# Last feed-forward layer of the first block in two halves of 256 tokens, the second interleaved with the expert rows

## The chip, the cores and the metric

One core of a Trainium2 chip runs the whole kernel. The metric is device time in microseconds. The runs shown took 3353.31, 3354.09 and 3354.44 us (median 3354.09); the profiled execution spans 3351.2 us from its first to its last instruction, 2.9 us less than the median.

## The reference

A model in fp32 on 512 tokens of width 1024. Two layers of a first block (a short convolution, then an SSD mixer, each followed by a SwiGLU layer of inner width 2816), then one hybrid layer (banded attention beside a gated delta rule, then product-key experts). What matters here:

```python
def swiglu_ffn(h, w_in, w_out):            # w_in 1024 x 5632, w_out 2816 x 1024
    gate, up = jnp.split(h @ w_in, 2, axis=-1)
    return (jax.nn.silu(gate) * up) @ w_out
# first block, end of each layer:
h = rmsnorm(x, norm_g[i, 2]) * (1.0 + scale) + shift
y = swiglu_ffn(h, f_w_in[i], f_w_out[i])
x = x + gate * rmsnorm(y, norm_g[i, 3])
# hybrid layer: x -> attention + delta rule -> x, then experts (16 of 16384 for each of 8 heads):
s1, s2 = ...                               # scores against 128 + 128 sub-keys, top 16 of each,
top_s, pos = lax.top_k(cand_s, 16)         # then top 16 of the 256 sums, for each head
u, vv = expert_down[experts], expert_up[experts]
act = jax.nn.gelu(jnp.einsum("thkd,td->thk", u, hb))
y = jnp.einsum("thk,thkd->td", gates * act, vv)
```

Attention and the delta rule look backwards only, so tokens 0 to 255 can pass through the hybrid layer before tokens 256 to 511.

## The kernel before

Activations stand transposed in SBUF: `xT` holds 8 tiles of 128 features x 512 tokens. Each engine has one program written out in order (`pe_program`, `act_program`, `dve_program`, `pool_program`, `sp_program`, L2522 to L2615); semaphores tie them together. There is no planner: the order of the generators' steps is the order of the work.

**Weights in pieces.** A piece is 128 x 1024 words (0.52 MB). SP loads all of them in one fixed order (`LOADS`, L382 on) into four raw slots; a slot is loaded again when its last reader has finished. Among the pieces up to the last feed-forward layer stand 144 loads of modulation weights, of late one to every two pieces; VectorE multiplies them by a vector (`dve_ada`). For the first block a piece is split in two fp32r parts: ACT copies it to a rounded tile (`act_ahead`, L400), VectorE subtracts that copy (`dve_ahead`, L412), three tiles of each deep. `pe_gemm` (L461) then runs 24 matmuls a piece: high x high, high x low, low x high for each of its 8 tiles. The hybrid layer takes its pieces in fp32 straight from the raw slots (`pe_plain`), and for each half of 256 tokens, so these pieces are loaded twice.

**The last feed-forward layer** (`pe_pre`, `pe_ffn`, `pe_out` with index 3): norm over all 512 tokens, 44 gate and up pieces with 512 moving columns, the gated products of all 22 inner tiles kept in SBUF in two parts, then 22 pieces' worth of output weights in the order output tile by output tile (24 shorter pieces), each output tile squared and copied out while the next one is computed. GpSimd adds the squares up (`pool_out`).

**The hybrid layer by halves.** `pe_main(e, f)` (L2240) and its ACT and VectorE counterparts are generators: norm 8 steps (for f = 1 only 2, as the root is computed beforehand by `act_norm_squares`, `pool_norm_sum`, `pe_norm_sum`, `act_norm_root`), projections 15, attention with the delta rule's projections 34 (for f = 1: 16 steps attention alone, then both), inverses 18, state 6, delta norm 5, output projection 9, norm 8, queries and key scores 20. Half 0 runs alone. In its last steps VectorE begins to rank chunk 0 (a chunk is 128 tokens; `dve_topk`, 33 steps a chunk).

**The expert rows.** 512 rows: row n takes one expert for each of the 128 tokens of a chunk, 128 rows a chunk. GpSimd gathers a row's down and up weights (1.05 MB) by an indirect DMA into a ring of slots (`pool_gather`, L2336): 7 slots, from row 150 on 4 more (memory of attention and delta rule, once free), from 260 on one more. VectorE takes the dot with the token (L187, 1024 wide), ACT applies Gelu and the gate and builds a diagonal matrix, TensorE adds the weighted up row to PSUM banks 0 and 1 (`pe_add`, two fp32 matmuls of 512 columns, four records); for rows chosen by `own_add` VectorE adds instead (`dve_add`). A slot is free when its row is added.

**The interleave.** Before the rows, `before_rows` (L2453) does 9 ranking steps and 6 steps of half 1. Then, behind every second row, `steps_of` (L2460) makes one step of half 1 and in chunk 0 one or two ranking steps for chunk 1; when half 1 is through, ranking steps alone. On each engine a row's work and a step's work stand in one queue:

```python
for g, (c, grp) in enumerate(ALL_GROUPS):      # pe_experts
    ...
    if grp % 2:
        steps_of(c, grp // 2, main, ranks)
        next(late, None)
    if g:
        pe_add(e, *ALL_GROUPS[g - 1])
```

Half 1 has 117 steps, so its last step stands at row 222.

Line numbers in the profile are those of small helpers: L153 all matmuls, L164 all activations, L170 two-operand VectorE and GpSimd operations, L182 multiply-adds with a scalar, L187 the dots, L216 the gathers.

Of the kernel before, what the change touches and what calls it, by code (L numbers as in the profile page):

```python
# [226 lines left out]
def build(nc, t, out):  # L227
    ctx = ExitStack()
    with ctx:
# [53 lines left out]
        w_f, w_r = take_r(6144, LOW + 8192)  # L283
        raw_first = raw + [h_mem[:, 4096 + 1024 * i:5120 + 1024 * i] for i in range(4)]
# [38 lines left out]
        def ffn_pieces(layer, half):  # L323
            for kk in range(KF):
                for part in range(2):
                    piece(("ffn", half, kk, part), t["fin"][layer, 2 * kk + part])
            out_pieces(half, t["fout"][layer], FGROUPS)

        ffn_pieces(0, 1)
# [6 lines left out]
        ffn_pieces(1, 3)  # L336
        NSPLIT = len(PIECES)
        for f in range(2):
            for n in range(12):
                piece(("qkv", f, n), t["win2"][n])  # L340
# [9 lines left out]
        NP = len(PIECES)  # L350

# [26 lines left out]
        def w_tile(p):  # L378
            i = 2048 * (p % 3)
            n = 128 * PIECES[p][1]  # L380
            return i, n

        def sp_load(e, i):
            kind, n = LOADS[i]
            s = slot_of(i)
            if former(i) >= 0:
                old, m = LOADS[former(i)]
                if old == "w":
                    e.wait_ge(*(w_lo.at(m) if m < NSPLIT else gemm.at(m)))
                else:  # L390
                    e.wait_ge(*ada_step.at(m))
# [8 lines left out]
        def act_ahead(e):  # L400
            p = nxt["act"]
            if p >= NSPLIT:
                return
            nxt["act"] += 1
            i, n = w_tile(p)
            e.wait_ge(*w_in.at(("w", p)))
            if p >= 3:
                e.wait_ge(*gemm.at(p - 3))
            e.act(w_r[:, i:i + n], raw[slot_of(NUMBER["w", p])][:, 0:n], ACT.Copy).then_inc(*w_hi.tick(p))

        def dve_ahead(e):
            while nxt["dve"] < len(LOADS):  # L412
# [6 lines left out]
                if p >= NSPLIT:  # L419
                    return  # L420
                i, n = w_tile(p)
                e.wait_ge(*w_hi.at(p))
                e.tt(w_r[:, i + 1024:i + 1024 + n], raw[slot_of(a)][:, 0:n], w_f[:, i:i + n],
                     ALU.subtract).then_inc(*w_lo.tick(p))
# [36 lines left out]
        def pe_gemm(e, p, o, rhs, k0=0, start=True, stop=True, ready=None, own=None):  # L461
            i, n = w_tile(p)
            k = n // 128
            hi, lo = tiles(w_r[:, i:i + n], k), tiles(w_r[:, i + 1024:i + 1024 + n], k)
# [765 lines left out]
        mixd = H[:, 0:4, :]  # L1230
        Sst = room(512)
        qT = tiles(room(1024), 4)
        kT, vtok = [tiles(room(2048), 4) for _ in range(2)]
        over = room(8704)
        htk = [room(1024) for _ in range(2)]
        fin_out = room(1024)
        lvl = tiles(room(896), 7)
# [24 lines left out]
        SB = [over[:, 2048:4096], over[:, 0:2048]]  # L1262
        nine = lambda a: [a[:, 512 * i:512 * i + 512] for i in range(9)]
        kv_mem = tail[:, 3584:7680]
# [26 lines left out]
        n1_sq, n1_add, n1_pe = [signal(n) for n in ("half_squares", "half_sum", "half_total")]  # L1291
# [36 lines left out]
        def x_half(i, f, k):  # L1328
            return x_new(3, k) if i == 4 else ps.done(("wo", f, k))
# [28 lines left out]
        n1_sum, n1_log = fin_out[:, 0:512], fin_out[:, 512:768]  # L1358
        n1_part = [fin_out[:, 512:1024], n1_sum]

        def act_norm_squares(e):
            for m in range(4):
                e.wait_ge(*x_half(4, 1, 2 * m + 1))
                if m > 1:
                    e.wait_ge(*n1_add.at(m - 1))
                e.act(pairs(n1_part[m == 0]), xT[:, 2 * m:2 * m + 2, half_of(1)], ACT.Square).then_inc(*n1_sq.tick(m))

        def pool_norm_sum(e):
            for m in range(1, 4):
                e.wait_ge(*n1_sq.at(m))  # L1370
                if m > 1:
                    e.wait_ge(*n1_add.at(m - 1))
                e.tt(n1_sum, n1_sum, n1_part[0], ALU.add).then_inc(*n1_add.tick(m))

        def pe_norm_sum(e):
            o = ps.claim("n1", HB)
            e.wait_ge(*ps.vacant("n1"))
            e.wait_ge(*n1_add.at(3))
            e.mm(o[:, 0:256], ones, n1_sum[:, 0:256], True, False)
            e.mm(o[:, 0:256], ones, n1_sum[:, 256:512], False, True).then_inc(*n1_pe.tick(0))  # L1380

        def act_norm_root(e):
            e.wait_ge(*n1_pe.at(0))
            e.act(n1_log, ps["n1"][:, 0:256], ACT.Ln, bias=cc("eps"), scale=1.0 / D).then_inc(*ps.release("n1"))
            e.wait_ge(*ps.done("n1"))
            e.act(n1_log, n1_log, ACT.Exp, scale=-0.5).then_inc(*rs_ok.tick(("tn", 4, 1)))

        def act_norm_shift(e):
            for s in range(2):
                for k in range(4 * s, 4 * s + 4):  # L1390
                    e.wait_ge(*dve_b.at(("tn", 4, 1, k)))
                    e.act(hrows(k), hrows(k), ACT.Identity, bias=shift(4, k)).then_inc(*t_h.tick((4, 1, k)))
                yield

        def dve_norm_scale(e):
            for s in range(2):
                for k in range(4 * s, 4 * s + 4):
                    e.wait_ge(*der_ok.at((4, "pre")))
                    e.wait_ge(*rs_ok.at(("tn", 4, 1)))
# [1352 lines left out]
```

## Time and profile before

| stage | us |
|---|---|
| median of the runs | 3354.09 |
| span of the profiled execution | 3351.2 |
| last feed-forward layer's pieces | 1160 to 1530 |
| first half of the hybrid layer | 1549.4 to some 1893 |
| first gather issued | 1854.2 |
| dots of the 512 rows | 1914.3 to 3341 |
| TensorE busy, share of the span | 2945.8, 88% |
| VectorE busy | 2119.7, 63% |
| ACT busy | 1400.0, 42% |
| DMA moved | 797.82 MB, of these 536.90 by the gathers |

The shares are means over stages that differ: most of the transfers fall into the last 1500 us, in which TensorE is less busy than before.

### The profile page before, as it was taken

The numbers are of one execution on the slowest core, as the hardware profiler recorded it, in microseconds if no ns is written. First come the engines' busy times: TensorE is split into PE (matmuls) and PEld (weight loads), VectorE is DVE, ScalarE is ACT, GpSimd is POOL, SyncE is SP. The second block draws the span as 40 slices with busy tenths as digits, with TensorE's granted clock in tenths as the row PEclk, the third lists the DMA queues.
The fourth block names the chain that finished last, engine by engine and source line by source line (L and its number), as shares of the span: only waits on it lengthen the run. The fifth ranks groups of instructions, "written<-read, shape, count | busy, mean of one in ns | idle before, by whom it ended". The sixth has DMA issues, their size and how long they took to land.

```text
span 3351.2 us, 34609 instructions
## 1 busy us (share of the span) xinstructions
PE 2945.8 (88%) x11990; PEld 2050.0 (61%) x11990; DVE 2119.7 (63%) x3960; ACT 1400.0 (42%) x2879; POOL 652.5 (19%) x575
## 2 busy tenths in 40 slices
PE   6989999899998899998988998878879777777777
PEld 5868888688776688887777753656547232223222
DVE  7655443587786444432552999879669889655555
ACT  3243222444665422224733367772443433333333
POOL 0000000000111000000000133334443444443442
PEclk8999999999998999998998999989989899999999
DMA  6544444244122244442202597989999999999998
GB/s 251 184 144 135 142 141 145 85 151 132 58 70 95 95 139 148 144 129 98 98 26 87 220 371 267 355 341 387 412 420 417 353 421 422 421 422 421 421 421 335
DMA packets 147548, 797.82 MB, mean 238 GB/s; under 512 B 16304, under 2 KB 18480, under 8 KB 81712
## 3 DMA queue, kind: packets, MB, share of 16 engines
q0 software_dynamic: 73728, 536.90, 39.5%
q1 hardware_dynamic: 69840, 251.69, 22.6%
q10 hardware_dynamic: 3808, 7.02, 0.6%
q8 instruction: 97, 1.59, 0.2%
q14 instruction: 75, 0.61, 0.0%
HBM read 793.46 MB, written 2.10 MB: 237 GB/s over the span
## 4 chain that ended last, share of the span: by engine, by line
PE 52%; DMA 20%; DVE 18%; ACT 6%; issue 4%; POOL 0%; DVEq 0%; SPq 0%; POOLq 0%; ACTq 0%
PE psum L153 51%; DMA tail<-in_experts,tail 19%; DVE tail L187 5%; DVE tail L170 2%; ACT L164 2%; DVE tail L182 2%; ACT arena L164 2%; DVE tail L193 1%; DVE arena L182 1%; DVE tail L190 1%; DVE region L170 1%; DVE rounded L170 1%; ACT tail L164 1%; DVE tail L205 1%; DVE tail L196 1%
## 5 line engine op out<-in xcount | busy, mean ns | idle before, releaser
L153 PE MATMUL psum<-tail,arena 128*128 128x256 f32 (+2 forms) x3584 | 1274.5, 505 | 256.2 <-ACT arena L164 235.5
L153 PE MATMUL psum<-rounded,rounded 128*128 128x512 f32 x5496 | 1278.6, 393 | 39.6 <-DVE rounded L182 22.6
L153 PEld LDWEIGHTS psum<-rounded,rounded 128*128 128x128 f32 x5496 | 1034.0, 189 | 262.5 <-issue 29.0
L153 PEld LDWEIGHTS psum<-tail,arena 128*128 128x128 f32 x3584 | 677.7, 199 | 806.1 <-issue 748.4
L187 DVE CUSTOM_DVE_ANT_0 tail<-tail 128x1024 f32<-128x1024 f32 x512 | 621.0, 1223 | 311.7 <-DMA tail<-in_experts,tail 310.4
L216 POOL DMA_INDIRECT tail<-in_experts,tail x512 | 583.6, 1140 | 1015.9 <-PE psum L153 747.0
L164 ACT ACTIVATE tail<-tail 128x1 f32<-128x1 f32 (+1 forms) x1057 | 266.8, 252 | 769.2 <-DVE tail L187 740.7
L170 DVE TENSOR_TENSOR rounded<-arena,rounded 128x1024 fp32r<-128x1024 f32 (+2 forms) x285 | 316.5, 1111 | 333.7 <-ACT rounded L164 333.5
L164 ACT ACTIVATE rounded<-arena 128x1024 fp32r<-128x1024 f32 (+2 forms) x317 | 292.1, 939 | 406.5 <-DVE arena L170 232.5
L164 ACT ACTIVATE arena<-psum 128x256 f32<-128x256 f32 (+2 forms) x210 | 97.5, 480 | 393.6 <-PE psum L153 392.9
L170 POOL TENSOR_TENSOR arena<-arena 128x512 f32<-128x512 f32 x32 | 47.1, 1473 | 1087.7 <-ACT arena L164 1087.7
L164 ACT ACT_TABLE_LOAD x192 | 246.3, 1283 | 13.8 <-PE psum L153 8.3
L182 DVE SCALAR_TENSOR_TENSOR arena<-arena 128x512 f32<-128x512 f32 (+1 forms) x294 | 213.0, 727 | 21.4 <-issue 10.4
L153 PE MATMUL psum<-arena 128*128 128x1 f32 (+3 forms) x712 | 156.5, 345 | 58.6 <-ACT arena L164 40.7
L164 ACT ACTIVATE arena<-arena,tail 128x128 f32<-128x128 f32 x428 | 172.2, 402 | 14.0
L153 PEld LDWEIGHTS psum<-arena 128*128 128x128 f32 x712 | 109.5, 201 | 102.3 <-issue 61.9
L153 PE MATMUL psum<-tail 128*128 128x128 f32 (+4 forms) x888 | 138.4, 302 | 22.5 <-DVE tail L182 13.2
L153 PEld LDWEIGHTS psum<-tail 128*128 128x128 f32 (+2 forms) x888 | 109.3, 188 | 57.4 <-issue 32.9
L170 DVE TENSOR_TENSOR arena<-psum,arena 128x512 f32<-128x512 f32 (+1 forms) x88 | 41.4, 474 | 156.2 <-PE psum L153 155.8
L182 DVE SCALAR_TENSOR_TENSOR arena<-psum,arena 128x511 f32<-128x511 f32 (+3 forms) x112 | 79.6, 711 | 57.9 <-ACT arena L164 30.9
L182 DVE SCALAR_TENSOR_TENSOR tail<-tail 128x1024 f32<-128x1024 f32 (+1 forms) x96 | 105.4, 1098 | 3.2 <-ACT tail L164 2.6
L170 POOL TENSOR_TENSOR region<-region 128x256 f32<-128x256 f32 x24 | 17.7, 737 | 363.6 <-DVE region L170 363.6
(87 smaller groups left out, 1560.4 us busy)
## 6 DMA issues: line engine op xcount, KB each, us to landing
arena<-in_ada SPq DMA_DIRECT2D x136, 512.0 KB, 3.7
arena<-in_fin SPq DMA_DIRECT2D x88, 512.0 KB, 4.2
arena<-in_win SPq DMA_DIRECT2D x56, 512.0 KB, 3.3
arena<-in_fout SPq DMA_DIRECT2D x32, 512.0 KB, 4.1
arena<-in_mxbc SPq DMA_DIRECT2D x32, 512.0 KB, 3.7
arena<-in_pq SPq DMA_DIRECT2D x32, 512.0 KB, 7.8
arena<-in_ain SPq DMA_DIRECT2D x24, 512.0 KB, 4.7
arena<-in_mz SPq DMA_DIRECT2D x16, 512.0 KB, 3.8
```

The source lines that it names most:

```text
L153: return self.e.matmul(o, a, b, start=start, stop=stop, skip_group_check=skip)
L164: return self.e.activation(o, a, func, bias=bias, scale=scale)
L170: return self.e.tensor_tensor(o, a, b, op)
L182: return self.e.scalar_tensor_tensor(out=o, in0=a, scalar=s, in1=b, op0=op0, op1=op1)
L187: return self.e.tensor_tensor_reduce(o, a, b, 1.0, 0.0, ALU.mult, ALU.add, total)
L190: return Unissued() if self.e is None else self.e.max(o, a)
L193: return Unissued() if self.e is None else self.e.max_index(o, m, a)
L196: return Unissued() if self.e is None else self.e.match_replace(o, m, a, -3.0e38)
L205: return Unissued() if self.e is None else self.e.tensor_reduce(o, a, AX_X, op)
L216: return self.e.indirect_dma_start(out=o, out_offset=None, in_=table, in_offset=bass.IndirectOffsetOnAxis(ap=rows, axis=0))
```

## The change

The last feed-forward layer is done for tokens 0 to 255 (`drive(pe_half(e, 0))`), then half 0 of the hybrid layer runs as before; the layer for tokens 256 to 511 (`pe_half(e, 1)`) is put in front of the steps of half 1 of the hybrid layer. All 66 pieces of the layer are loaded and split again for the second half, in tiles of their own (`w1_f`, `w1_r`). The output weights come row tile by row tile (`fout2`), 22 pieces of 8 output tiles; all eight output tiles (256 columns each) are summed at once in PSUM banks 4 to 7, from pair to pair of inner tiles, so the gated products of only two pairs are kept. A step of the half is one piece; there are 8 + 66 + 2 = 76. The norm in front of the hybrid layer's half 1 is now made by the ordinary 8 steps.

```diff
+        HALF = []
+        for j in range(KF // 2):
+            HALF += [("gate", 2 * j), ("gate", 2 * j + 1), ("up", 2 * j), ("up", 2 * j + 1)]
+            if j:
+                HALF += [("out", 2 * j - 2), ("out", 2 * j - 1)]
+        HALF += [("out", KF - 2), ("out", KF - 1)]
...
+            for what, kk in HALF:
+                SPLIT.append(len(PIECES))
+                piece(("half", f, what, kk), t["fout2"][kk] if what == "out" else t["fin"][1, 2 * kk + (what == "up")])
...
         def act_ahead(e):
...
+            e.wait_ge(*w_in.at(("w", p)))
+            if q >= AGAIN + 3 or 3 <= q < AGAIN:
+                e.wait_ge(*gemm.at(SPLIT[q - 3]))
+            if q >= AGAIN:
+                e.wait_ge(*gemm.at(pc["pq", 0, 15]))
+                e.wait_ge(*tk_pe.at((1, 1)))
...
+        def pe_half_out(e, f, kk):
...
+            a, b = a2r[:, j % 2, half_of(u)], b2r[:, j % 2, half_of(u)]
+            for d in range(8):
...
+                o = ps["hy", f, d // 2][:, half_of(d % 2)]
+                e.mm(o, hi[:, d, :], a, kk == 0 and d % 2 == 0, False, True)
+                e.mm(o, hi[:, d, :], b, False, False, True)
+                last = kk == KF - 1 and d % 2 == 1
+                ins = e.mm(o, lo[:, d, :], a, False, last, True)
...
+        def pe_half(e, f):
+            yield from pe_norm(e, 3, f)
+            for s, (what, kk) in enumerate(HALF):
+                p = pc["half", f, what, kk]
+                if what == "out":
+                    pe_half_out(e, f, kk)
+                else:
+                    key = what, f, kk // 2
+                    if kk % 2 == 0:
+                        ps.claim(key, (2,) if what == "gate" else (3,))
+                        e.wait_ge(*ps.vacant(key))
+                    pe_gemm(e, p, ps[key][:, half_of(kk % 2)], lambda k: (h2r[:, k, :], l2r[:, k, :]),
+                            ready=h_ready(f) if s == 0 else None)
+                pe_after(e, p, (0, 1))
+                yield
+            o = ps.claim(("hs", f), (2,))
+            e.wait_ge(*ps.vacant(("hs", f)))
+            for b in range(4):
+                pe_pair_stat(e, ("hs", f, b), o[:, 0:256], ones, b == 0, b == 3)
+            yield
+            yield
```

`act_half` and `dve_half` go with it: per step ACT splits the piece three ahead; per pair of inner tiles it applies Silu to 512 columns and copies the product to its high part, VectorE multiplies and subtracts (two operations of 512 columns). Behind the last piece ACT squares the four banks and copies the eight tiles out, and VectorE scales and adds them to `xT`.

```diff
-        SB = [over[:, 2048:4096], over[:, 0:2048]]
+        SB = [ring_mem[5], ring_mem[6], over[:, 2048:4096], over[:, 0:2048]]
...
-        FROM, FROM_LAST = 150, 260
-        turn_of, slot_no, last_use, prev = list(range(NRING)), [], {}, []
+        FROM_SEVENTH, FROM, FROM_LAST = 80, 190, 260
+        turn_of, slot_no, last_use, prev = list(range(NRING - 1)), [], {}, []
         for n in range(512):
+            if n == FROM_SEVENTH:
+                turn_of = [NRING - 1] + turn_of
...
-            if n < 192:
-                return s % 2 == 1 and (16 <= s if n >= 128 else 48 <= s < 124)
-            return 16 <= s < 124 and s % (8 if n < 256 else 16) == 1
+            return 16 <= s < 124 and s % (4 if n < 72 else 2 if n < 192 else 8 if n < 256 else 16) == 1
...
+                if n == NRING - 2:
+                    e.wait_ge(*idx_ok.at((0, 3)))
+                if n == FROM_SEVENTH:
+                    e.wait_ge(*idx_ok.at((1, 3)))
...
-        EARLY, LEFT = 6, 9
+        EARLY, LEFT = 8, 9
...
             if c < 2 and next(main, True) is None:
-                some(ranks, 1 + grp % 2 if c == 0 else 0)
-            else:
+                some(ranks, grp % 2 if c == 0 else 0)
+            elif grp % 2:
                 some(ranks, 2 if c == 1 else 1)
...
-            main = pe_main(e, 1)
+            main = both(pe_half(e, 1), pe_main(e, 1))
...
+                steps_of(c, grp, main, ranks)
                 if grp % 2:
-                    steps_of(c, grp // 2, main, ranks)
                     next(late, None)
...
-            pe_pre(e, 3)
-            pe_ffn(e, 3)
-            pe_out(e, 3, FGROUPS, arhs, a_at(3))
+            drive(pe_half(e, 0))
             drive(pe_main(e, 0))
```

So a step of half 1 now stands behind every row instead of every second one; the feed-forward half's 76 steps and the hybrid half's 123 end at row 191. The scores of chunks 0 and 1 lie in ring slots 5 and 6, which join the ring at gathers 5 and 80; the four slots of attention memory join at gather 190. Between rows 16 and 124 of a chunk VectorE adds every fourth row up to row 71, every second one up to row 191.

## Rows read from the trace of the kernel before

**Rows 1.** The page's slices, the whole span in 40 parts: DMA share, GB/s.

```profile
DMA  6544444244122244442202597989999999999998
GB/s 251 184 144 135 142 141 145 85 151 132 58 70 95 95 139 148 144 129 98 98 26 87 220 371 267 355 341 387 412 420 417 353 421 422 421 422 421 421 421 335
```

**Rows 2.** Windows: us, busy (count) of each engine, clock, DMA share, GB/s.

```profile
1160.00:1530.00 370.00, 370.00 (x1650) 306.62 (x1650) 154.13 (x188) 102.02 (x130) 7.77 (x6) 0.99 0.41 131
1530.00:1549.40 19.40, 8.45 (x20) 4.56 (x19) 11.02 (x21) 11.31 (x16) 0.00 (x0) 0.70 0.00 0
1549.40:1854.20 304.80, 276.71 (x1436) 234.68 (x1437) 130.92 (x336) 142.37 (x256) 3.87 (x3) 0.94 0.25 84
1854.20:1914.50 60.30, 53.69 (x276) 47.74 (x275) 55.69 (x203) 17.80 (x46) 6.72 (x7) 0.92 0.65 244
```

**Rows 3.** The same windows' view, stretches of the expert rows.

```profile
1914.50:1979.60 65.10, 62.80 (x215) 39.43 (x213) 59.17 (x170) 43.27 (x98) 22.91 (x20) 1.00 0.89 332
2090.60:2219.90 129.30, 112.04 (x430) 78.55 (x429) 106.92 (x214) 98.66 (x191) 43.24 (x37) 0.92 0.90 351
2219.90:2330.50 110.60, 88.91 (x483) 64.16 (x482) 98.80 (x151) 42.58 (x112) 50.41 (x38) 0.94 0.92 364
2481.30:2615.40 134.10, 124.26 (x512) 86.69 (x511) 113.67 (x297) 47.70 (x162) 51.50 (x42) 0.97 0.99 407
2695.20:3340.10 644.90, 491.98 (x1025) 182.01 (x1024) 402.89 (x796) 228.41 (x759) 264.56 (x247) 0.96 1.00 417
1914.50:2615.40 700.90, 602.23 (x2285) 379.29 (x2283) 589.07 (x1280) 375.43 (x903) 272.25 (x224) 0.94 0.93 367
```

**Rows 4.** The dots' line, three windows: count, duration, first and last start.

```profile
L187 DVE CUSTOM_DVE_ANT_0 tail<-tail x190: 1204/1221/1285, 1914.3 to 2503.3; 128x1024 f32<-128x1024 f32 x190
L187 DVE CUSTOM_DVE_ANT_0 tail<-tail x222: 1204/1221/1285, 1914.3 to 2615.2; 128x1024 f32<-128x1024 f32 x111
L187 DVE CUSTOM_DVE_ANT_0 tail<-tail x257: 1203/1226/1285, 2694.9 to 3340.0; 128x1024 f32<-128x1024 f32 x129
```

**Rows 5.** Groups by shape, 1914.5 to 2615.4 us: busy, mean ns, idle before.

```profile
L153 PE MATMUL psum<-tail,arena 128*128 128x512 f32 x616 | 312.5, 645 | 64.2 <-ACT arena L164 64.2
L182 DVE SCALAR_TENSOR_TENSOR tail<-tail 128x1024 f32<-128x1024 f32 x64 | 81.9, 1279 | 2.6 <-ACT tail L164 2.6
L164 ACT ACT_TABLE_LOAD x80 | 102.6, 1283 | 1.4
```

**Rows 6.** Groups by shape, the adds of 1914.5 to 1979.6 us.

```profile
L153 PE MATMUL psum<-tail,arena 128*128 128x512 f32 x80 | 36.1, 593 | 1.3 <-ACT arena L164 1.3
```

**Rows 7.** Groups by shape, TensorE: 1170 to 1380 us, last row 1721 to 1752.

```profile
L153 PE MATMUL psum<-rounded,rounded 128*128 128x512 f32 x907 | 207.2, 390 | 0.0
L153 PE MATMUL psum<-arena 128*128 128x1 f32 x40 | 4.7, 240 | 0.0
L153 PEld LDWEIGHTS psum<-rounded,rounded 128*128 128x128 f32 x906 | 169.7, 188 | 35.2
L153 PE MATMUL psum<-tail 128*128 128x128 f32 x250 | 30.1, 279 | 2.0 <-DVE tail L170 1.4
```

**Rows 8.** Groups by shape, VectorE and ACT, 1160 to 1390 us.

```profile
L170 DVE TENSOR_TENSOR rounded<-arena,rounded 128x1024 fp32r<-128x1024 f32 x40 | 48.8, 1222 | 42.8 <-ACT rounded L164 42.8
L182 DVE SCALAR_TENSOR_TENSOR arena<-arena 128x512 f32<-128x512 f32 x40 | 30.0, 750 | 0.7
L170 DVE TENSOR_TENSOR arena<-psum,arena 128x512 f32<-128x512 f32 x20 | 13.8, 692 | 53.5 <-PE psum L153 53.5
L164 ACT ACTIVATE rounded<-arena 128x1024 fp32r<-128x1024 f32 x40 | 41.9, 1047 | 0.0
```

**Rows 9.** Waits (total, times, longest): 1914.5 to 2503.3 us, last 2695.2 to 3340.1.

```profile
POOL tail L216 <- PE psum L153: 331.0, 116, 56.2
DVE tail L187 <- DMA tail<-in_experts,tail: 52.1, 39, 2.5
DVE tail L187 <- DMA tail<-in_experts,tail: 235.5, 191, 2.2
```

More of the change, by code:

```diff
@@ L321, in build @@
         out_pieces(0, t["aout"], GROUP)
[L323 to L329, printed above, removed]
+        for kk in range(KF):
+            for part in range(2):
+                piece(("ffn", 1, kk, part), t["fin"][0, 2 * kk + part])
+        out_pieces(1, t["fout"], FGROUPS)
         piece("dt", t["mdt"])
@@ L1230, in build @@
         mixd = H[:, 0:4, :]
+        qT = tiles(room(1024), 4)
+        over = room(8704)
+        lvl = tiles(room(896), 7)
+        y2 = tiles(tail[:, 2048:4096], 8)
+        kv_mem = room(4096)
+        kT, vtok = [tiles(kv_mem[:, 2048 * i:2048 * i + 2048], 4) for i in range(2)]
         Sst = room(512)
-        qT = tiles(room(1024), 4)
-        kT, vtok = [tiles(room(2048), 4) for _ in range(2)]
-        over = room(8704)
         htk = [room(1024) for _ in range(2)]
         fin_out = room(1024)
-        lvl = tiles(room(896), 7)
         keys = tiles(room(256), 2)
@@ L1388, in act_norm_shift @@
[L1388 to L1392, printed above, removed]
-                yield
[L1395 to L1399, printed above, removed]
-                    e.wait_ge(*tk_pe.at((1, 1)))
-                    e.wait_ge(*gemm.at(pc["pq", 0, 15]))
-                    e.stt(hrows(k), xT[:, k, half_of(1)], pre(4, k), n1_log, ALU.mult, ALU.mult).then_inc(
-                        *dve_b.tick(("tn", 4, 1, k)))
-                yield
+        h_ready = lambda f: lambda k: ga.done(("hb", f, k // 2))
@@ new lines, in build @@
+        gate_of_pair = lambda what, kk: kk // 2 if what == "gate" and kk % 2 else None
+        up_of_pair = lambda what, kk: kk // 2 if what == "up" and kk % 2 else None
+        hb = lambda f, k: ga["hb", f, k // 2][:, half_of(k % 2)]
+        def pe_half_out(e, f, kk):
+            p = pc["half", f, "out", kk]
+            j, u = kk // 2, kk % 2
+            _, hi, lo = [tiles(a, 8) for a in w_tile(p)]
+            e.wait_ge(*w_lo.at(p))
+            e.wait_ge(*ga.done(("hg", f, j)))
+            a, b = a2r[:, j % 2, half_of(u)], b2r[:, j % 2, half_of(u)]
+            for d in range(8):
+                if kk == 0 and d % 2 == 0:
+                    ps.claim(("hy", f, d // 2), (4 + d // 2,))
+                    e.wait_ge(*ps.vacant(("hy", f, d // 2)))
+                o = ps["hy", f, d // 2][:, half_of(d % 2)]
[3 more added lines that the diff above has]
+                ins = e.mm(o, lo[:, d, :], a, False, last, True)
+                if last and d < 7:
+                    ins.then_inc(*hy_ok.tick((f, d // 2)))
+            ins.then_inc(*gemm.tick(p))
@@ new lines, in dve_half @@
+        def dve_half(e, f):
+            if f == 0:
+                dve_derived(e, 3)
+                dve_derived_post(e, 3)
+            for s in range(8):
+                if s == 5 or f and s in (3, 4):
+                    dve_ahead(e)
+                for k in range(4 * (s - 6), 4 * (s - 6) + 4) if s >= 6 else ():
+                    e.wait_ge(*h_hi.at((3, f, k)))
+                    ins = e.stt(l2r[:, k, :], hb(f, k), shift(3, k), h2f[:, k, :], ALU.add, ALU.subtract)
+                    if k % 2:
+                        ins.then_inc(*ga.release(("hb", f, k // 2)))
+                for k in range(4 * (s - 5), 4 * (s - 5) + 4) if s in (5, 6) else ():
+                    if k % 2 == 0:
+                        e.wait_ge(*ga.vacant(("hb", f, k // 2)))
+                    e.wait_ge(*der_ok.at((3, "pre")))
+                    e.wait_ge(*x_half(3, f, k))
+                    e.wait_ge(*rs_ok.at(("tn", 3, f)))
+                    e.stt(hb(f, k), xT[:, k, half_of(f)], pre(3, k), rst[0][:, 0:256], ALU.mult, ALU.mult).then_inc(
+                        *dve_b.tick(("tn", 3, f, k)))
+                yield
+            made = None
+            for s, (what, kk) in enumerate(HALF):
+                if made is not None:
+                    dve_half_low(e, f, made)
+                if s + 3 < len(HALF):
+                    dve_ahead(e)
+                made = up_of_pair(what, kk)
+                if made is not None:
+                    g = ga["hg", f, made]
+                    e.wait_ge(*ps.done(("gate", f, made)))
+                    e.wait_ge(*gemm.at(pc["half", f, what, kk]))
+                    e.tt(g, ps["up", f, made], g, ALU.mult).then_inc(*ps.release(("up", f, made)))
+                dve_after(e, pc["half", f, what, kk])
+                yield
+            yield
+            e.wait_ge(*rs_ok.at(("hs", f)))
+            for b in range(5):
+                if b < 4:
+                    y = y2[:, 2 * b:2 * b + 2, :]
+                    e.wait_ge(*ps.done(("hy", f, b)))
+                    e.tt(y, y, rst[1][:, 0:256].unsqueeze(1).broadcast_to([128, 2, 256]), ALU.mult).then_inc(
+                        *y_sc.tick((3, f, b)))
+                if b:
+                    x = xT[:, 2 * b - 2:2 * b, half_of(f)]
+                    e.wait_ge(*y_sc.at((3, f, b - 1)))
+                    e.tt(x, x, y2[:, 2 * b - 2:2 * b, :], ALU.add).then_inc(*x_ok.tick((3, f, b - 1)))
+            yield
@@ L2607, in pool_program @@
             pool_ssd(e)
-            for i in range(2, 4):
-                pool_out(e, i)
-            pool_norm_sum(e)
+            pool_out(e, 2)
             pool_gather(e)
```

181 lines of the change are left out of this document (103 added, 78 removed).

## The prediction

> **What bounds the kernel now.** I read the slices first [rows 1]: up to some 1840 us (slice 22 of 40) the DMA engines stand mostly at two to four tenths, from 2260 us (slice 28) on at nine or more until the end, mostly at 412 to 422 GB/s. The stages follow in the windows: the layer's 66 pieces at 1160 to 1530 us keep TensorE busy for all of 370 us; then comes the first half of the last layer, and 60.3 us in which VectorE is busy for 55.7 with ranking chunk 0 [rows 2]. The first expert row is read at 1914.3 us, the 190th at 2503.3, the 222nd at 2615.2, the 512th at 3340.0 [rows 4]. So rows 256 to 512 take 644.9 us or 2.52 us each, at a DMA share of 1.00 (rows 222 to 512: 724.7 us, 2.50 each): a row of 1.05 MB at 421 GB/s is 2.49. There VectorE waits 235.5 us for gathers [rows 9]; nothing but fewer bytes or an earlier start shortens it. Ahead of row 222 the second half of the layer runs between the rows: 700.9 us, TensorE busy for 602.2 (0.859), DMA share 0.93 [rows 3]. Up to row 190 VectorE waited only 52.1 us for gathers, while the gather queue waited 331.0 us for TensorE to free a slot [rows 9]. That stretch is bound by compute, and the change puts its work there.
>
> **The change, by parts. a) Pace of a 256-column step.** Each piece still needs 24 matmuls, each with a 128x128 weight load, but moves 256 columns. The trace has no such fp32r matmul. The 512-column ones take 365 us / (66 x 24) = 230 ns (370 less some 5 us of small products) [rows 2]. Nearest rows: with one column a weight load and matmul take 4.7/40 = 117 ns; 128 columns of fp32 (two passes, so 256 cycles at 2.4 GHz, 107 ns) take 30.1/250 = 120 ns, 122 with the gaps; half of 230 is 115. Bounds: 115, and 187, the mean recorded length of a load (169.7/906) if it can't overlap [rows 7]. I take 122 ns, by the 128-column row: 2.94 us for a piece, 194 us for 66, against 365.
> The Trainium skill (TensorE: Matmul & The Clock Gate, LDWEIGHTS) gives a load as its columns over 1.2 GHz, 107 ns, and its gap for 256 columns is 109; the sum by that would be 43 us lower over both halves. The one-column row (117) doesn't reach 107, so I stay with the rows.
> Feeding the pieces: a split costs ACT 1.05 us and VectorE 1.22. With 0.75 us of modulation work per piece (two operations, one weight in two) and 0.25 of gating (two of 0.69 us in six pieces) VectorE needs 2.2 of 2.94 us [rows 8]; loads come at 1.5 x 0.52 MB per piece, 270 GB/s. Hidden; a raw slot is free 2.3 us behind a piece's end and its next weights are due some 8 us behind it, so it would cost once a load took over 5.5 us.
>
> **b) First half.** Norm as before (first piece some 1 us later, and paced by the eight norm outputs: +5), 194 + 5 us of pieces, then the tail: all eight output tiles end together now, so squares, their sum, root, scaling, add and the next norm lie on the path. Before, it was 19.4 us [rows 2]; two more roots and squares against shorter operations: 21 (17 to 28). First projection matmul at 1160 + 1 + 5 + 199 + 21 = 1386 us instead of 1549.4: 163 us gained. The attention half behind it is unchanged (scores go to ring slots 5 and 6).
>
> **c) Start of the rows.** Ranking chunk 0 bounds the 60.3 us. Added there on VectorE: 16 operations of the half norm and three weight subtractions, less 8 scalings: some 7 us. Four projection pieces that TensorE did beside the ranking move behind it (counted in e). Row 1 at 1914.5 - 163 + 7 = 1758.5 us. The gather ring begins with five slots instead of seven; as five rows have landed long before row 1, I cost it at nothing (0 to 6 us).
>
> **d) Rows 0 to 67, with the 66 pieces.** One step a row now, eight steps before the rows. 13 of these rows are added by VectorE, 55 by TensorE at 36.1/20 = 1.80 us [rows 6]. TensorE: 194 + 99 = 293 us; at the 0.965 of the densest stretch now (62.8 of 65.1 us) [rows 3] 304 us, and 8 for the last two steps: 312. Beside it per row: VectorE 1.22 + 0.08 for the dot, 1.22 for the subtraction, 1.0 of ranking chunk 1 (half a step a row; 25 steps and some 7 us of norm filled the 55.7), 0.25 of own adds (13 x 1.28 / 68) [rows 5], 0.23 of gating, together 4.0 of 4.6 us; DMA 2.49 + 1.25 = 3.7. Both under TensorE, VectorE not by much. ACT: 11 times Silu between Gelus, 22 table loads of 1.28 us [rows 5], covered. Moved past SP's queue: 66 loads of 0.52 MB more, 34.6 MB, 82 us at 421 GB/s; hidden only while the DMA isn't the bound.
> The Trainium skill (Trainium Kernel Development and Optimization, Key Constraints) says that transfers issued by SP, ACT and POOL share the same 16 DMA engines and interleave. The trace agrees: 407 GB/s with weight loads among the gathers and 417 without [rows 3].
>
> **e) Rows 68 to 190, with attention, delta rule and queries.** 123 steps, 123 rows, 73 of them added by TensorE. TensorE's part without rows: 602.2 less the adds' 312.5 [rows 3, 5] is 290, and 15 for the four pieces moved in: 305. Adds 73 x 1.80 = 131. Sum 436. At the share 0.859 that it reaches over these stages now [rows 3] 508 us; the stages of waits (two norms, row update) had two rows a step to fill them and have one: +8. 516. Bottom: 436 at a full TensorE. Top: 545 at 0.80, which is the invert stage's share now (88.9 of 110.6).
> The waits that the diff adds: gather 80 for chunk 1's ranks (ready by row 66, nothing); gather 5 for chunk 0's last ranks (before row 1, nothing); gather 190 instead of 150 gets the four more slots, and its wait ends at row 148. The conv step's wait for chunk 1's ranks goes; it had long been over.
>
> **f) Rows 191 to 512.** Bound by gathers as now. A ring that TensorE holds back stands full, six rows ahead: (322 - 6) x 2.51 = 793 us, between the 2.50 and 2.52 above [rows 4]. Then 11.2 us from the last dot to the end, as now.
>
> **Sum.** Row 1 to row 190 takes P = 312 + 516 = 828 us, against 588.8. End: 1758.5 + 828 + 793 + 11.2 = 3391 us against a span of 3351.2. The runs stand 2.9 us over the span (3354.09), so 3394 us: 1.2% slower. In one line: 163 less 7 gained before the rows, 239 lost up to row 190, 44 won back behind it. The saving on the path falls short, since all pieces are issued twice and the second time they stand in the one stretch where TensorE is already the limit; the DMA, which bounds the rest, idles meanwhile (631 us of transfers, 190 x 2.49 + 127 x 1.25, in 828).
>
> **Rivals.** 1) Faster: the row's adds fall into the gaps of the steps. Without rows the first attention half has TensorE busy 276.7 of 304.8 us [rows 2]; if one row per step just fills what is free, e) runs at 0.965 instead of 0.859: 452 us, P = 764, time 3330. It decides at P = 788; below that the kernel is faster. For it: one add per step is half the disturbance, chunk 1's ranking has left these stages, and after 2330 us part of the 0.859 is DMA-bound waiting. Against: stretches with a DMA share below 0.93 show 0.87 (112.0 of 129.3) and 0.80 as well [rows 3], where engines wait for each other inside a step.
> 2) VectorE becomes the bound of d): in-order, at 4.0 us a row with the share of 0.86, 4.65 becomes 5.0 with a wait of TensorE for the subtracted weights: +26, 3420.
> 3) The weight load doesn't overlap at 256 columns: 187 instead of 122 ns, twice 103 us, 3600. Against: the 120 ns row.
> 4) Only the columns count: 115 ns, twice 11 us, 3371; by the skill's 109 it would be 3351. The one-column row speaks against both.
> 5) The second half isn't done in time (the change doesn't overlap as it says): 76 + 123 steps less 8 end at row 191, chunk 2's last five ranking steps by row 201, gather 256 asks for them at about row 245. No cost; it would cost one 2.5 us for each row beyond that.
>
> **How the numbers follow.** Forecast 0.56, with 3360 to 3430 of its own; rival 1 0.24; rival 2 0.09; rival 3 0.03; rival 4 0.07; rival 5 0.01. A measurement of this kernel tells 0.2% (7 us) from no change. Faster by more: nearly all of rival 1 and a little of 4, 0.24; within it, where P lies at 781 to 795: 0.08; slower 0.68. The range takes in rival 1 and the top of e) with rival 2: 3320 to 3445.
>
> **What would show it.** The fp32r groups with 128x256: 120 to 125 ns busy per matmul (a and b right), 187 (rival 3). First projection matmul at 1386 and first dot at 1759 us. Dot 68 some 312 us and dot 190 some 828 us behind the first; DMA share in between 0.75, not 0.92; gathers waiting for TensorE for well over 331 us, VectorE for gathers hardly at all. From dot 190 on 2.5 us a row. The prediction is wrong if dot 190 comes before 2547 us (1758.5 + 788), or if rows 68 to 190 hold TensorE at over 0.93.

## The result, and the profile after

The kernel with the change takes 3463.12 us (median of 4 runs, 3461.55 to 3463.80) against 3354.27 (4 runs, 3353.31 to 3354.48) on the same chip: a ratio of 1.0325, 95% interval 1.031 to 1.034. The forecast was 3394 us with a range up to 3445: slower, as forecast, but by 109 us instead of 40. The profiled execution spans 3459.7 us.

The slices of after, of the same 40 parts as [rows 1]:

```profile
DMA  6534444243213485411467777877897999999998
GB/s 252 183 129 143 140 142 150 88 144 110 67 62 122 154 267 176 135 62 49 164 232 281 285 283 305 342 254 250 313 364 280 422 422 421 421 422 421 422 421 333
```

The rows begin in slice 21. From there to slice 31 the DMA engines stand mostly at seven and eight tenths; the nines and the 421 GB/s of the bound by gathers begin with slice 32 (2681 us) only. Before they began at slice 28, at 387 GB/s.

Windows of after (us, busy and count of each engine, clock, DMA share, GB/s), for [rows 2, 3]: the first half's pieces and its tail, then the rows up to the 68th dot, to the 190th, to the 200th, to the 256th and to the last.

```profile
1162.00:1362.00 200.00, 199.21 (x1649) 198.94 (x1650) 135.32 (x163) 83.04 (x94) 0.00 (x0) 0.99 0.75 244
1362.00:1382.00 20.00, 10.64 (x39) 8.40 (x38) 8.05 (x17) 15.49 (x28) 0.00 (x0) 0.81 0.00 0
1749.30:2108.70 359.40, 303.69 (x1773) 238.07 (x1771) 251.28 (x490) 161.67 (x301) 81.03 (x65) 0.94 0.78 281
2108.70:2637.90 529.20, 471.69 (x2078) 335.84 (x2078) 391.97 (x807) 315.00 (x661) 145.30 (x130) 0.94 0.82 309
2637.90:2674.80 36.90, 14.85 (x19) 5.41 (x20) 33.33 (x93) 14.90 (x35) 8.38 (x7) 0.64 0.57 194
2674.80:2802.50 127.70, 99.09 (x203) 37.29 (x202) 76.67 (x120) 48.44 (x164) 66.54 (x59) 0.96 1.01 421
2802.50:3449.00 646.50, 491.41 (x1026) 181.90 (x1025) 403.29 (x796) 229.12 (x759) 266.35 (x247) 0.96 1.00 416
```

The line of the dots in two windows of after, for [rows 4] (first and last start):

```profile
L187 DVE CUSTOM_DVE_ANT_0 tail<-tail x190: 1154/1220/1249, 1748.9 to 2637.5; 128x1024 f32<-128x1024 f32 x190
L187 DVE CUSTOM_DVE_ANT_0 tail<-tail x68: 1205/1220/1228, 1748.9 to 2108.4; 128x1024 f32<-128x1024 f32 x68
```

Against before: row 1 is read 165 us earlier, rows 1 to 190 take 888.6 us instead of 589.0 (+300), rows 190 to 512 811 instead of 837 (-26), and the end behind the last dot is 11 us in both: +109 together. The bill that doesn't fit is in the first window of rows. TensorE is busy for 303.7 of 359.4 us, 0.845, where the forecast had 293 of 304 and 8 us of an ending. The chain of waits of that stretch, by line:

```profile
by line: DVE tail L187 21.1%; ACT rounded L164 18.5%; issue 17.6%; DVE rounded L170 11.9%; ACT tail L164 9.5%; DVE tail L193 4.9%; DVE tail L190 4.3%; DVE tail L170 3.9%; DVE tail L196 2.8%; DVE arena L170 2.1%; DVE tail L205 1.6%; DVE tail
```

TensorE (PE psum L153) isn't among its first eleven. ("issue" is time in which an engine waited for nothing that the profile shows.) What is: dots on VectorE, weight copies on ACT (rounded L164), Gelu and gate on ACT (tail L164), subtractions on VectorE (rounded L170). Two rows of it in the timeline of after (start, duration, what; idle time and its releaser in brackets):

```profile
1903.81 1.21 DVE L187 CUSTOM_DVE_ANT_0 tail<-tail 128x1024 f32<-128x1024 f32 x1
...
1905.05 0.53 ACT L164 ACTIVATE tail<-tail 128x1 f32<-128x1 f32 x2 [5.27 <-DVE tail L187]
1905.62 0.40 ACT L164 ACTIVATE arena<-arena,tail 128x128 f32<-128x128 f32 x1
1905.92 1.04 ACT L164 ACTIVATE rounded<-arena 128x1024 fp32r<-128x1024 f32 x1
1906.16 2.91 PE L153 MATMUL psum<-tail,arena 128*128 128x512 f32 x4 [2.14 <-ACT arena L164]
1907.00 1.23 DVE L170 TENSOR_TENSOR rounded<-arena,rounded 128x1024 fp32r<-128x1024 f32 x1 [1.98 <-ACT rounded L164]
...
1908.14 1.22 DVE L187 CUSTOM_DVE_ANT_0 tail<-tail 128x1024 f32<-128x1024 f32 x1
...
1911.06 1.23 DVE L170 TENSOR_TENSOR rounded<-arena,rounded 128x1024 fp32r<-128x1024 f32 x1 [1.69 <-ACT rounded L164]
...
1915.03 1.23 DVE L187 CUSTOM_DVE_ANT_0 tail<-tail 128x1024 f32<-128x1024 f32 x1
```

It reads as a ring of two engines. The dot ends; ACT does Gelu and gate (0.53) and the diagonal (0.40) and, behind them in its queue, the copy of the piece three ahead (1.04); VectorE waits for that copy, subtracts it (1.23), and only then comes to the next dot, whose row had long landed. Dot to dot is 4.33 us with nothing else in it. Between the next two dots stands a ranking step as well: 6.89. Both rows together take 11.2 us, for which TensorE has one add (VectorE adds the second row itself) and two pieces, some 7.7 us by the paces of [rows 6] and the 120 ns below. Here it is at them for 9.3 us, since after its wait of 2.14 us its clock is granted at half from 1907.0 to 1910.4 us. So TensorE looks nearly full, but part of that is the price of its waits; whether it bounds is a question for the experiments. The waits of rows 1 to 68 of after (total, times, longest) show its two seams and what they do to the others, for [rows 9]:

```profile
POOL tail L216 <- PE psum L153: 195.2, 53, 7.8
ACT tail L164 <- DVE tail L187: 172.0, 67, 5.4
DVE rounded L170 <- ACT rounded L164: 101.1, 63, 2.0
PE psum L153 <- ACT arena L164: 54.3, 26, 4.1
```

VectorE waits for the copy 63 times, 1.6 us each time: once in every piece. TensorE waits for the diagonal, its clock is granted at 0.94 on average, and the gather queue waits for TensorE to free a slot. No dot of these rows waits for a gather, so the missing slot of the ring isn't the cause.

### The profile page after: what moved, and what is told of

The parts are those of the page before. It is cut to its first block, busy times and chain, and to the rows that moved or that the text cites. A ratio compares the mean times of both kernels' runs of the same rounds, so it can differ in the third digit from the quotient of the medians.

```text
span 3459.7 us, 38183 instructions
## 1 busy us (share of the span) xinstructions
PE 2988.4 (86%) x13622; PEld 2147.5 (62%) x13622; DVE 2204.3 (64%) x4042; ACT 1509.4 (44%) x2991; POOL 630.7 (18%) x566
## 4 chain that ended last, share of the span: by engine, by line
PE 48%; DVE 18%; DMA 18%; ACT 12%; issue 5%; POOL 0%; DVEq 0%; SPq 0%; ACTq 0%; POOLq 0%
PE psum L153 47%; DMA tail<-in_experts,tail 17%; DVE tail L187 4%; ACT L164 3%; ACT tail L164 2%; DVE rounded L170 2%; ACT rounded L164 2%; ACT arena L164 2%; DVE tail L170 2%; DVE tail L193 1%; DVE arena L182 1%; DVE tail L190 1%; DVE tail L182 1%; DVE region L170 1%; DVE tail L196 1%
## 5 line engine op out<-in xcount | busy, mean ns | idle before, releaser
L153 PE MATMUL psum<-tail,arena 128*128 128x256 f32 (+2 forms) x3572 | 1284.6, 506 | 306.1 <-ACT arena L164 284.1
L153 PE MATMUL psum<-rounded,rounded 128*128 128x512 f32 (+1 forms) x7080 | 1338.8, 349 | 57.8 <-DVE rounded L182 41.0
L153 PEld LDWEIGHTS psum<-rounded,rounded 128*128 128x128 f32 x7080 | 1133.6, 192 | 250.3 <-issue 73.8
L153 PEld LDWEIGHTS psum<-tail,arena 128*128 128x128 f32 x3572 | 666.6, 198 | 838.1 <-issue 777.1
L164 ACT ACTIVATE tail<-tail 128x1 f32<-128x1 f32 (+1 forms) x1056 | 267.6, 253 | 853.2 <-DVE tail L187 823.0
L170 DVE TENSOR_TENSOR rounded<-arena,rounded 128x1024 fp32r<-128x1024 f32 (+2 forms) x349 | 397.2, 1138 | 372.5 <-ACT rounded L164 372.0
L164 ACT ACTIVATE rounded<-arena 128x1024 fp32r<-128x1024 f32 (+3 forms) x389 | 363.6, 949 | 385.5 <-DVE arena L170 171.0
L164 ACT ACTIVATE arena<-psum 128x256 f32<-128x256 f32 (+1 forms) x210 | 97.2, 480 | 325.3 <-PE psum L153 324.4
L182 DVE SCALAR_TENSOR_TENSOR arena<-arena 128x512 f32<-128x512 f32 (+2 forms) x302 | 214.0, 714 | 19.5 <-issue 8.4
L153 PE MATMUL psum<-arena 128*128 128x1 f32 (+3 forms) x772 | 169.8, 349 | 59.8 <-ACT arena L164 47.6
L153 PEld LDWEIGHTS psum<-arena 128*128 128x128 f32 x772 | 123.7, 205 | 102.1 <-issue 64.8
L164 ACT ACTIVATE arena<-arena,tail 128x128 f32<-128x128 f32 x426 | 171.9, 403 | 13.9
L170 POOL TENSOR_TENSOR arena<-arena 128x512 f32<-128x512 f32 x26 | 39.4, 1514 | 708.4 <-ACT arena L164 708.4
L153 PE MATMUL psum<-tail 128*128 128x128 f32 (+4 forms) x888 | 137.1, 300 | 15.8 <-DVE tail L182 9.7
L153 PEld LDWEIGHTS psum<-tail 128*128 128x128 f32 (+2 forms) x888 | 107.6, 185 | 46.5 <-issue 26.0
L182 DVE SCALAR_TENSOR_TENSOR arena<-psum,arena 128x511 f32<-128x511 f32 (+3 forms) x112 | 79.7, 711 | 74.0 <-PE psum L153 40.8
L182 DVE SCALAR_TENSOR_TENSOR tail<-tail 128x1024 f32<-128x1024 f32 (+1 forms) x98 | 108.2, 1104 | 5.3 <-ACT tail L164 4.4
L164 ACT ACTIVATE arena<-psum,arena 128x512 f32<-128x512 f32 (+1 forms) x70 | 48.6, 694 | 100.8 <-PE psum L153 100.4
L170 DVE TENSOR_TENSOR arena<-psum,arena 128x512 f32<-128x512 f32 (+1 forms) x88 | 41.2, 471 | 80.2 <-PE psum L153 79.8
```

What stands on the lines that cost most here:

```text
L153: return self.e.matmul(o, a, b, start=start, stop=stop, skip_group_check=skip)
L164: return self.e.activation(o, a, func, bias=bias, scale=scale)
L170: return self.e.tensor_tensor(o, a, b, op)
L182: return self.e.scalar_tensor_tensor(out=o, in0=a, scalar=s, in1=b, op0=op0, op1=op1)
```

## The experiments

Theory A: this ring bounds the rows that carry the second half's pieces. Rival B: TensorE is the bound after all, its pieces and adds being slower among each other than the sum had them. (From e4 on, the theories that the expectations call A and B are named anew each time; A is mostly the view that fits the runs before it.) All ratios are to the kernel before on the same chip.

**e1: the subtraction one step later.** ACT still copies three pieces ahead; VectorE subtracts two ahead.

```diff
-                if s + 3 < len(HALF):
+                if (s and s + 2 < len(HALF)) if f else s + 3 < len(HALF):
                     dve_ahead(e)
```

> Edit: in the second half VectorE subtracts the weights of the piece two ahead, one step behind ACT's copy of it, instead of the piece three ahead in the same step. Nothing is left out. Theory A (a loop between VectorE and ACT sets rows 1 to 68: dot 1.2 us, Gelu and gate 0.55, diagonal 0.4, ACT's copy of the weights 1.05, VectorE's subtraction 1.2, then the next dot, and every second row a ranking step of some 2 to 3 us inside it; VectorE stands 101 us before 63 subtractions): those waits go, dot 1 to dot 68 falls from 359 us to 300 to 320, the time from 3463 to 3405 to 3430. Theory B (TensorE is the bound there and only fills badly, by its slow clock and by the steps' own latencies): within 8 us of 3463.

Measured: 3382.44 us, ratio 1.0084 (1.0067 to 1.0101). Windows, waits and chain of e1, rows 1 to 68:

```profile
1748.70:2029.10 280.40, 277.64 (x1772) 226.32 (x1771) 247.87 (x490) 161.52 (x301) 87.80 (x66) 1.00 0.94 360
```

```profile
DVE rounded L170 <- ACT rounded L164: 14.5, 12, 2.6
```

```profile
by line: PE psum L153 92.5%; DVE tail L187 1.4%; issue 1.2%; DVE rounded L170 1.0%; DVE tail L170 1.0%; DVE tail L205 0.6%; DVE tail L182 0.5%; ACT tail L164 0.5%; ACT L164 0.5%; DVE arena L170 0.2%; ACT arena L164 0.2%; DVE tail L199 0.2%;
```

The same work (x490 instructions on VectorE in both) take 280.4 us instead of 359.4. TensorE is busy for 99% of it at a full clock and makes up 92.5% of the chain. One step of slack between two in-order queues was worth 79 us in these rows, 81 of the 109 us in the end. That is more than A had expected (stretch 300 to 320 us).

**e2: fewer matmuls, the ring left.** The low x high product of the second half is left out (a third of its matmuls; its loads, copies and subtractions stay).

```diff
+                if p in SECOND:
+                    ins = e.mm(o, hi[:, i, :], b, False, stop and i == k - 1)
+                else:
...
+                if f:
+                    ins = e.mm(o, hi[:, d, :], b, False, last, True)
```

> Left out: in the second half the third product of every piece (low part of the weights times high part of the activations), 16 matmuls instead of 24; loads, copies, subtractions and order stay. TensorE gets 66 x 8 x 0.120 = 63 us less to do in rows 1 to 68. Theory A (the loop between VectorE and ACT sets the pace): dot 1 to 68 shrinks by 5 to 25 us of 359, the time falls to 3438 to 3458. Theory B (TensorE): by 50 to 63 us, 3400 to 3413.

Measured: 3462.04 us, 1.032 (1.0303 to 1.0338), within 1.1 us of after. Rows 1 to 68 of e2:

```profile
1749.60:2108.90 359.30, 257.16 (x1250) 184.02 (x1248) 251.47 (x490) 161.50 (x301) 77.27 (x66) 0.88 0.79 282
```

523 matmuls fewer, and the stretch is 0.1 us shorter. TensorE waits for diagonals 99.1 instead of 54.3 us and its clock falls from 0.94 to 0.88. B is out; A had expected 5 to 25 us.

**e3: no adds on VectorE in these rows** (`own_add` false below row 72).

```diff
-            return 16 <= s < 124 and s % (4 if n < 72 else 2 if n < 192 else 8 if n < 256 else 16) == 1
+            return not n < 72 and 16 <= s < 124 and s % (4 if n < 72 else 2 if n < 192 else 8 if n < 256 else 16) == 1
```

> Edit: of the rows below 72 VectorE adds none, TensorE adds all (14 rows more, 1.8 us each; VectorE 14 x 1.28 us less). Nothing is left out. Theory A: VectorE's adds lie in the loop, so dot 1 to 68 shrinks by 8 to 18 us, the time to 3445 to 3455. Theory B: TensorE has 25 us more, the time rises to 3480 to 3488.

Measured: 3468.54 us, 1.0338 (1.0321 to 1.0356), rows 1 to 68 in 362.2 us. That fits neither expectation. VectorE lost 14.6 us of work and waited 17 us more for copies (118.1 instead of 101.1): an own add had stood where VectorE would have waited anyway. TensorE took on twelve adds (319.6 us busy) without becoming the bound.

**e4: no second half** (its 76 steps are empty, its loads left out).

```diff
-            for what, kk in HALF:
+            for what, kk in HALF if f == 0 else ():
...
-            main = both(pe_half(e, 1), pe_main(e, 1))
+            main = both(wait_steps(76), pe_main(e, 1))
```

> Left out: the feed-forward layer for tokens 256 to 511, with its 66 loads; its 76 steps between the rows are empty, everything else stands where it stood. It prices the second half where the change put it. Both theories: rows 1 to 68 go at the gathers' pace, 68 x 2.5 = 170 us instead of 359, a few us of start (half norm) less, rows 68 to 190 within 10 us of their 529: time 3260 to 3280, so the second half costs 183 to 203 us between the rows. Before the change the full width cost 172 us more than the half width does in front (389.4 against 217.5 from the first piece to the first projection): a price above 172 means that the interleave itself loses. Rival: rows 68 to 190 gain over 20 us too (3250 or less), because the ring would arrive there full.

Measured: 3262.15 us, 0.972 (0.9704 to 0.9736). Windows of e4, rows 1 to 68 and 68 to 190:

```profile
1740.00:1913.10 173.10, 116.57 (x213) 42.80 (x213) 161.59 (x405) 57.96 (x192) 81.07 (x65) 0.88 0.97 395
1913.10:2443.60 530.50, 473.73 (x2062) 337.37 (x2062) 387.27 (x799) 305.16 (x644) 146.19 (x129) 0.93 0.82 308
```

The second half costs 201 us where it stands now, more than the 172 that its tokens had cost in front before the change (389.4 us at full width against 217.5 at half): the interleave itself loses. With the ring gone (e1) it costs 120. Rows 68 to 190 take 530.5 us without it and 529.2 with it: that stretch owes nothing to the pieces.

**e8: e1 and e2 together** (one run, made after e7).

> On top of e1, left out: the third product of every piece of the second half, as in e2. In the changed kernel taking 63 us off TensorE gave 1 us. Theory A (the loop hid it; with the loop gone TensorE bounds): rows 1 to 68 fall from 280 us to 245 to 260, where VectorE (248 busy) and the DMA (0.94) bound; time 3345 to 3362. Theory B (TensorE's work never mattered there): 3378 to 3385.

Measured: 3362.7 us in the one run; rows 1 to 68 in 257.5 us, TensorE busy for 225.4, VectorE for 246.6. With the ring gone, the matmuls that brought 1 us bring 20 (A's stretch, and 0.7 us above its time), and then VectorE is nearly full.

**e7: e1 with an own add in every third row instead of every fourth** (`3 if n < 72`).

> On top of e1: of the rows below 72 VectorE adds every third instead of every fourth (18 or 19 instead of 14). With the loop gone TensorE is busy for 277.6 of the 280.4 us of rows 1 to 68, VectorE for 248. Theory A (TensorE bounds there now): 5 rows x 1.8 us less for it, 5 to 9 us gained, 3373 to 3377. Rival (VectorE's order bounds as soon as it is over nine tenths busy): no gain or up to 5 us lost.

Measured: 3382.76 us, 1.0085 (1.0069 to 1.0102). Rows 1 to 68 became 6.8 us shorter, as A had it. But row 1 came 1.8 us later and rows 68 to 190 took 5.3 us longer, so nothing is left. The time is the rival's, its reason isn't; why the later rows gave the gain back stays open.

**e5 and e6: the steps spread.** e5 is e1 and leaves out every fourth step place in rows 128 to 211; e6 also takes the four slots of attention's memory from row 172 on instead of 190.

```diff
         def steps_of(c, grp, main, ranks):
+            if c == 1 and grp % 4 == 3 and grp < 84:
+                return
```

> On top of e1 (subtraction one step later, 3382 us): in chunk 1 every fourth row gets no step of the second half, so its last step stands at row 212 instead of 191. Nothing is left out. Theory A (rows 68 to 190 are bound by TensorE's work of steps and adds, 472 of 529 us busy, while behind row 190 the gathers bound and TensorE is a quarter idle): some 21 rows' adds come in among the steps instead of behind them, beside gathers that go on; behind row 212 only 300 rows are left at 2.5 us. 20 to 35 us gained, 3347 to 3362. Theory B (what bounds rows 68 to 190 is the length of each step's own chain of waits, so a row without a step costs its own 2.5 us and no more is gained): 0 to 8 us gained, 3374 to 3382.

> e5_spread with the four more ring slots from gather 172 on instead of 190. Both theories: a ring that TensorE holds back isn't short of slots, so within 5 us of e5_spread. Rival: the ring of seven slots is what leaves the DMA at 0.82 in rows 68 to 190; then 5 to 15 us less than e5_spread.

Measured: 3360.17 us, 1.0016 (1.0007 to 1.0026), and 3359.09 us, 1.0016 (1.0006 to 1.0026). e5 lies in A's range, and B is out. In e1 the steps ended at row 191, with the gathers idle a fifth of the time before and sole bound behind. Spread, rows 1 to 190 take 750 us instead of 810 and rows 190 to 512 848 instead of 811. The slots brought nothing that can be told. These two are the best forms found, still 5 us behind the kernel before.

**e9: e6 with own adds in every second row up to row 215** (`2 if n < 216`).

> The order of e6 (subtractions a step later, every fourth step of the first rows left out, four more gather slots from 172 on), and VectorE adds every second row up to row 215 instead of 191; nine or ten adds of 1.8 us leave TensorE. Theory A (TensorE is the bound between rows 68 and 215, VectorE loosely tied by now): rows 190 to 215 took 108.8 us in e5 (4.35 each) and become 90 to 95, the end 10 to 18 us earlier, 3341 to 3350 us. Rival (VectorE's last ranking steps for chunk 2 bound these rows): no gain, 3356 to 3362 us.

Measured: 3371.74 us, 1.0058 (1.0044 to 1.0072): 13 us slower than e6, worse than the rival. I had read that TensorE is busy for 102 of 109 us in rows 190 to 215 of e6. The chain of that stretch of e6 says who sets its time:

```profile
by line: DMA tail<-in_experts,tail 21.9%; DVE tail L187 21.7%; DVE tail L193 17.1%; DVE tail L190 14.0%; DVE tail L170 10.6%; DVE tail L196 9.0%; issue 6.1%; DVE tail L182 3.8%; DVE tail L205 3.8%; DVE tail L199 1.5%; DVE tail L176 1.2%; DV
```

VectorE and the gathers; TensorE isn't among its first eleven. Nine more adds of 1.28 us (12 us) went to VectorE in rows 193 to 215. In e9's chain of the stretch the adds (DVE tail L182) have 9.7% instead of 3.8, 7 us more, and the stretch took 118.6 us instead of 109.1.

**e10, e11: ten pieces moved ahead of the rows** (on top of e9: two steps of the second half behind each of the nine ranking steps), with two of three or three of four step places used.

> As e9, with two steps of the second half of the layer instead of one behind each of the nine ranking steps ahead of the rows (18 steps: 8 of the norm and 10 pieces), and two of three step places used up to row pair 80. Ahead of the rows TensorE was busy for 36 of 59 us. Theory A: ten pieces of 2.9 us move under the ranking; row 1 comes 10 to 16 us later (ten more subtractions of 1.22 us on VectorE, which ranks there), rows 1 to 190 take 25 to 35 us less: 10 to 20 us below e9, 3325 to 3340 us. Rival (VectorE bounds the start, and what is gained behind is lost in front): within 5 us of e9.

> As e10, but three of four step places used (the pace of e9), so the steps end some ten rows earlier, at about row 199. Theory A: rows up to 68 as in e9, last steps past by row 199 so that the gathers alone bound the rest sooner; within 8 us of e10. Rival (the pace matters since the ring runs empty where steps are dense): 8 to 15 us above e10.

Measured: 3385.09 us, 1.0095 (1.008 to 1.0111), and 3385.67, 1.0096 (1.008 to 1.0111). Row 1 came at 1770.5 and 1768.3 instead of 1749.8, and only 8 and 4 us of it had come back by row 256. TensorE's gaps ahead of the rows (in e9 it is busy for 37 of 60 us) aren't free: VectorE, at 54 of 60, carries the subtractions. That fits the rival of e10, with a higher price than it named (13 us over e9); the pace (e11) made no difference.

**e12: e6 with the half's norm behind row 1** (`EARLY` 0, and every fourth place left out up to row 180).

> The order of e6, but none of the eight steps of the second half's norm ahead of the rows (they come behind rows 1 to 8), and of the step places of chunk 1 every fourth is left out up to row 180 only instead of 212, so that the steps end at about the same row. Theory (VectorE bounds the start, and the norm's steps hold little work of TensorE's): row 1 comes 5 to 9 us earlier than in e6 (1747.4), at about 1740, as in e4 whose second half is empty; behind it the norm's steps cost TensorE little, rows 1 to 512 take 0 to 8 us more: 3351 to 3359 us. Rival: the norm's steps are chains of waits between engines, and behind the rows each costs a row its cover: rows 1 to 68 take 10 us more or over, 3361 to 3370 us.

Measured: 3371.15 us, 1.0053 (1.0039 to 1.0067). Row 1 came 10 us earlier (1737.4), rows 1 to 190 took 7 us more, rows 190 to 215 122.9 instead of 109.1, where the steps now stand denser beside VectorE's ranking. Neither expectation; two things were changed at once, so what each cost stays open.

## Why the prediction was right and wrong

The direction and the front were right, the size was not, and the step that failed is d). By its own steps:

- **a) right.** A run of 192 matmuls with their loads in the timeline of after:

```profile
1179.83 23.28 PE L153 MATMUL psum<-rounded,rounded 128*128 128x256 f32 x192
```

The next group starts 23.1 us later: 120.4 ns each (122 forecast; 187 in rival 3, 115 and 109 in rival 4). Rivals 3 and 4 fall.
- **b) and c) right, 9 us pessimistic.** First projection matmul at 1380.1 (1386), first dot at 1749 (1758.5). The ring's fewer slots cost nothing that shows: no dot of rows 1 to 68 waits for a gather. What the second half adds ahead of row 1 is 9 us by e4 (1740.0) rather than 7.
- **d) wrong: 359 instead of 312 us, +47, and most of the 69 us that the forecast missed.** The step that failed is "both under TensorE, VectorE not by much". Its terms were near: TensorE was busy for 304 us against 293 (278 in e1, at a full clock), VectorE for 251 against 272 (68 x 4.0). What was missing is the order. The step compared each engine's sum with TensorE's and never laid one row's chain across VectorE and ACT: dot, gate, diagonal, copy, subtraction, next dot, 4.3 us before any ranking step. The share of 0.965 was borrowed from a stretch whose steps hold no split. e1 gives the number that the step would have had without the ring: 280.4 us, TensorE at 0.99, so 304 was even pessimistic. Rival 2 came nearest: it named VectorE's order and the subtracted weights. But it priced them at +26, with VectorE busy for 4.0 of 5.0 us a row; it was busy for 3.7 of 5.3, and the wait that counted was VectorE's own for the copy (101 us), not TensorE's for the subtracted weights (1 us).
- The Trainium skill (TensorE: Matmul & The Clock Gate, Architectural detail: the array is 16× 32×32, not 1× 128×128) says that ACT and VectorE are strict FIFO queues and only TensorE pulls weight loads ahead. The trace agrees: the 1.04 us copy starts behind the diagonal at 1905.92 and not when its raw weights had landed (they were issued at 1886.00 and had landed by 1889.6; ACT sat idle for 5.27 us ahead of the Gelu with that copy behind it), and VectorE's next dot stands behind the subtraction.
- **e) right in size, 529 against 516,** by two misses that nearly cancel. TensorE was busy for 471.7 us, not 436 (74 adds at 2.1 us instead of 1.8, and 316 us of steps instead of 305), at a share of 0.89 instead of 0.859. e4 shows the same 530 without any second half. Rival 1 asked for 452. The adds of these rows in after:

```profile
L153 PE MATMUL psum<-tail,arena 128*128 128x512 f32 x296 | 155.8, 653 | 28.0 <-ACT arena L164 22.5 <-issue 5.5
```

- **f) 811 instead of 793, +18.** The ring did stand ahead: rows 200 to 256 took 2.28 us each, under the pace of the gathers. But rows 190 to 200 took 3.7 each, with TensorE busy for 15 of 37 us and VectorE for 33: chunk 2's ranking comes two steps to every second row as soon as the second half is through. That is read from the windows and not tested by itself. The lead made up for these rows and no more: (322 - 6) x 2.51 should have been 322 x 2.52.
- **Signs that came for another reason.** Over rows 1 to 190 the gathers waited 532.8 us for TensorE ("well over 331") and the DMA share was 0.80 (0.75 forecast), as if TensorE were the limit. In rows 1 to 68 it was itself held back; a slot is late whichever engine delays the add.
- **Luck in the total.** Without the ring (e1) the kernel takes 3382 us, only 12 from the forecast, but by misses that cancel: the start 10 us early, d) 32 below 312, e) 14 over 516, f) 18 over 793.

So of the 109 us, 81 were the ring between VectorE and ACT (e1), 22 the density of the steps ahead of a stretch that gathers bound (e5), and 5 are left (e6): in the profiles 167 us saved in front against 174 more for the rows. The break-even at P = 788 didn't hold either: e5 has P = 750 and is still slower. It pays 37 us back behind row 190 against e1, and the break-even had taken the 793 us behind it as fixed. Whether another order could gain isn't shown.

## What to carry to other kernels

When work is put between other work on in-order engines, sum each engine, and then write one period's chain across the engines as well: what the second engine does for the first, in whose queue it stands, and what the first does before it may go on. Where a producer and a consumer stand on two queues that both carry another loop, give them a step of slack (here one line, 81 us). A busy share tells nothing of it: read the chain of the stretch, and read it again before moving work from the engine that looks full.

## What the runs showed of the hardware

- TensorE's granted clock fell as its waits grew. In rows 1 to 68 it was 1.00 in e1 (no waits for diagonals), 0.94 in after (54.3 us of them), and 0.88 in e2 (99.1 us), where a third of the pieces' matmuls were gone; of the 63 us (523 x 120 ns) that e2 took out, the busy time fell by only 47. The add's four records took a mean of 592 ns in e1, 678 in after and 730 in e2 (99.6 us busy for 53 adds in e1, 1.9 each).
- A piece directly behind an add was recorded at 3.42 us, not 2.9, in after and in e1 alike. But the piece starts 1.3 us behind the add's start in e1, so from there to the piece's end it is some 4.7 us, as the sum of both (1.80 + 2.94) had it.
